# RWKV-7 layer: the next head pair's key products stand inside the triangular level loop, GpSimd splits their weights at the pair's start, ScalarE stages them level by level

## What is computed

```python
up = jnp.pad(u, ((0, 0), (1, 1), (0, 0)))
xx = 0.5 * (up[:, :-2] + up[:, 2:]) - u
xr, xw, xk, xv, xa, xg = [u + xx * mu[j] for j in range(6)]
r = heads(xr @ w_rkv[0])
k = heads(xk @ w_rkv[1])
v = heads(xv @ w_rkv[2])
...
def step(S, inp):
    r_t, w_t, k_t, v_t, a_t, b_t = inp
    sa = jnp.einsum('bhvk,bhk->bhv', S, a_t)
    S = S * w_t[:, :, None, :] + sa[..., None] * b_t[:, :, None, :] + v_t[..., None] * k_t[:, :, None, :]
    return S, jnp.einsum('bhvk,bhk->bhv', S, r_t)
```

## Time and profile before

| | us |
|---|---|
| median of three runs | 2406.75 |
| lowest and highest run | 2403.61, 2407.95 |
| the profiled execution | 2404.21 |
| its span in the trace | 2402.4 |

### The profile page before, as it was taken

One profiled execution on the slowest core, in us unless ns is written; L12 is line 12 of the kernel. 1 busy time (PEld: TensorE's weight loads), 2 busy tenths in 40 slices (PEclk: granted clock), 3 DMA queues, 4 the chain that ended last, 5 costly groups with the idle time before them and its releaser, 6 DMA issues.

```text
span 2402.4 us, 56559 instructions
## 1 busy us (share of the span) xinstructions
PE 2294.2 (95%) x24506; PEld 1851.0 (77%) x24506; DVE 1560.0 (65%) x1761; ACT 1264.5 (53%) x1400; POOL 231.8 (10%) x222
## 2 busy tenths in 40 slices
PE   8999999999999889888988889999999999999998
PEld 4677676888888466666766778888888888888886
DVE  2544776222233855555555268888888888888898
ACT  3422024222222844444444267777787778787875
POOL 2000552000000041111101130000000000000010
PEclk8999999999999989999999999999999999999999
DMA  7556225333222411111110289999999999999994
GB/s 272 193 210 245 71 88 158 88 105 87 97 97 89 144 58 59 58 58 41 54 46 20 95 321 374 365 385 361 383 361 385 360 384 358 385 363 381 360 390 174
DMA packets 228487, 511.90 MB, mean 213 GB/s; under 512 B 15271, under 2 KB 108223, under 8 KB 228031
## 3 DMA queue, kind: packets, MB, share of 16 engines
q1 hardware_dynamic: 225470, 498.61, 56.9%
q10 hardware_dynamic: 1730, 7.10, 0.8%
q0 software_dynamic: 1152, 4.19, 0.5%
HBM read 492.58 MB, written 17.30 MB: 212 GB/s over the span
## 4 chain that ended last, share of the span: by engine, by line
PE 91%; DVE 3%; issue 3%; ACT 1%; DMA 1%; POOL 0%; SPq 0%; DVEq 0%; ACTq 0%; POOLq 0%
PE bank L1673 26%; PE bank L1703 13%; PE bank L1199 3%; PE bank L1200 3%; PE bank L1201 3%; PE bank L1339 2%; PE bank L1313 2%; PE bank L1076 2%; PE bank L1105 2%; PE bank L1077 2%; PE bank L1078 2%; PE bank L1350 2%; PE bank L1217 2%; PE bank L1216 2%; PE bank L1218 2%
## 5 line engine op out<-in xcount | busy, mean ns | idle before, releaser
L3060 DVE TENSOR_TENSOR w_low<-expert_w,w_high 128x1792 fp32r<-128x1792 f32 (+2 forms) x384 | 771.9, 2024 | 120.7 <-ACT w_high L2213 118.1
L2213 ACT CAST w_high<-expert_w 128x1792 fp32r<-128x1792 f32 (+2 forms) x384 | 652.0, 1701 | 217.0 <-PE bank L1673 144.5
L1673 PE MATMUL bank<-w_high,xg_high 128*128 128x448 f32 x1024 | 294.1, 368 | 4.0 <-DVE xg_low L3050 4.0
L1673 PE MATMUL bank<-w_high,xg_low 128*128 128x448 f32 x1024 | 293.1, 367 | 0.0
L1673 PE MATMUL bank<-w_low,xg_high 128*128 128x448 f32 x1024 | 293.1, 367 | 0.0
L1673 PEld LDWEIGHTS bank<-w_high,xg_high 128*128 128x128 f32 x1024 | 191.6, 189 | 21.3 <-DVE xg_low L3050 4.1
L1673 PEld LDWEIGHTS bank<-w_high,xg_low 128*128 128x128 f32 x1024 | 192.8, 188 | 17.0
L1673 PEld LDWEIGHTS bank<-w_low,xg_high 128*128 128x128 f32 x1024 | 192.9, 188 | 15.8
L1703 PE MATMUL bank<-w_high,hid_high 128*128 128x512 f32 x448 | 175.8, 392 | 0.0
L1703 PE MATMUL bank<-w_high,hid_low 128*128 128x512 f32 x448 | 174.9, 390 | 0.0
L1703 PE MATMUL bank<-w_low,hid_high 128*128 128x512 f32 x448 | 174.7, 390 | 0.0
(11 more groups left out here) (440 smaller groups left out, 4035.1 us busy)
## 6 DMA issues: line engine op xcount, KB each, us to landing
expert_w<-in_moe_w_dram SPq DMA_DIRECT2D x128, 1792.0 KB, 9.2
expert_w<-in_moe_w_dram SPq DMA_DIRECT2D x32, 2048.0 KB, 10.4
arena<-in_mod_w_dram SPq DMA_DIRECT2D x48, 1024.0 KB, 8.2
expert_w<-in_moe_w_dram SPq DMA_DIRECT2D x32, 1536.0 KB, 9.7
arena<-in_ffn_w_dram SPq DMA_DIRECT2D x44, 512.0 KB, 5.0
slot_rows<-arena SPq DMA_DIRECT2D x25, 512.0 KB, 5.4
arena<-in_hy_w_in_dram SPq DMA_DIRECT2D x12, 1024.0 KB, 5.3
arena<-in_rw_w_rkv_dram SPq DMA_DIRECT2D x48, 256.0 KB, 2.7
```

The source lines that it names most:

```text
L1673: last = pe.matmul(bank[b0 + v][:, 0:EH], x[:, k, :], w_[:, kk, v * EH:v * EH + EH], start=(k == 0 and x is XGH and w_ is wh), stop=(k == ...
L2213: act.copy(high_piece(kind, n), piece(kind, ering[q % ERN], n // 2, n % 2))\
L3060: dve.tensor_tensor(piece(kind, low[s], n // 2, n % 2), piece(kind, ering[s], n // 2, n % 2), high_piece(kind, n).bitcast(F32), ALU.subtract)\
```

## The change

- TensorE: the 24 key products of the next pair leave their block behind the bonus sum. In each round of the level loop stand six of them (two channel tiles, three products), ahead of `level_first`. They accumulate onto bank 2. A round waits for the staged weights of its level and for the clearing of bank 2. The signal that the keys are done is given by the first transpose of `Bt` behind the loop. The waits for `score_copy_h` move from ahead of the loop into `level_first`. The first decay product moves ahead of the rates.
- VectorE: behind the first key mask it clears bank 2 with a memset of 128x512.
- ScalarE: two copies of 128x256 for each level bring the weights of two channel tiles into `stage_high` and `stage_low`. The pair for level 0 stands ahead of the score copies and waits for GpSimd's `next_digits(i)`. The others stand behind the two `first_copy` of the level before. `key_copy` moves from behind `z_copy_1` to the place behind the last `first_copy` of the loop, and reads bank 2. TensorE's `last_second` waits for it.
- GpSimd: `next_digits(i)` moves to the very start of `pair(i)`, and waits for the last state product of pair i - 1 in place of the levels of pair i.
- SP: the next pair's key weights are loaded when the keys of the pair before are done; the other weights still wait for its gate product.

The core of the diff:

```diff
-            def ahead_keys(j, tiles):
-                if tiles[0] == 0:
-                    step(pe, "ahead_pool", "next_digits", j - 1)
-                for k in tiles:
-                    mm(bank[4][:, :], keys_w_high[:, k, :], keys_high[k], start=(k == 0), stop=False)
-                    mm(bank[4][:, :], keys_w_high[:, k, :], keys_low[k], start=False, stop=False)
-                    last = mm(bank[4][:, :], keys_w_low[:, k, :], keys_high[k], start=False, stop=(k == KT - 1))
-                if tiles[-1] == KT - 1:
-                    last.then_inc(sem("ahead_products"), one("ahead_products", "keys"))
+            def ahead_keys(i, lv):
+                step(pe, "pair_vectors", "keys_cleared", i)
+                pe.wait_ge(sem("ahead_copies"), staged_keys(i + 1, lv))
+                settle(pe)
+                for n in range(2):
+                    tokens, rest = (v[n][:, bass.ds(lv * T, T)] for v in (keys_high_part, keys_low_part))
+                    for w, x in ((stage_high, tokens), (stage_high, rest), (stage_low, tokens)):
+                        mm(bank[2][:, :], w[:, n, :], x, start=False, stop=True, skip_group_check=True)
...
             def ahead_rate(j):
...
+                ahead_decay(j, 0)
                 step(pe, "pair_copies", "z_copy_1", j - 1)
...
-                for h in range(2):
-                    step(pe, "pair_copies", f"score_copy_{h}", i)
-                settle(pe)
                 with pe.Fori(0, LOOPED) as lv:
+                    if more:
+                        ahead_keys(i, lv)
                     for h in range(2):
-                        level_first(h, lv * 2 + (PER_PAIR * i + h + 1))
+                        level_first(h, lv * 2 + (PER_PAIR * i + h + 1), i)
...
+                if more:
+                    step(pe, "ahead_copies", "key_copy", i + 1)
                 for h in range(2):
                     last_second(h, i)
...
                 if more:
-                    ahead_keys(i + 1, range(KT))
                     ahead_rate(i + 1)
-                    ahead_decay(i + 1)
+                    ahead_decay(i + 1, 1)
...
+                def stage_keys(lv):
+                    act.copy(stage_high, keys_w_high[:, lv::LOOPED, :])
+                    act.copy(stage_low, keys_w_low[:, lv::LOOPED, :])\
+                        .then_inc(sem("ahead_copies"), one("ahead_copies", f"keys_staged_{lv}"))
...
+                if more:
+                    step(act, "ahead_pool", "next_digits", i)
+                    stage_keys(0)
                 for h in range(2):
                     step(act, "pair_vectors", f"joined_0_{h}", i)
...
             def pair(i, more):
+                if more:
+                    step(pool, "pair_products", "out_sum", i - 1)
+                    settle(pool)
+                    next_digits(i)
                 step(pool, "ahead_vectors", "r_1", i)
...
-                if more:
-                    pool.wait_ge(sem("level_turned"), PER_PAIR * (i + 1))
-                    next_digits(i)
...
+                    if h == 0:
+                        step(dve, "pair_vectors", "keys_masked_0", i)
+                        dve.memset(bank[2][:, :], 0.0).then_inc(sem("pair_vectors"), one("pair_vectors", "keys_cleared"))
```

64 lines of the change are left out of this document (43 added, 21 removed).

## The result

The changed kernel took 2428.86 us in the median of four runs (2425.45 to 2435.16), the kernel before 2406.84 us beside it (2403.61 to 2407.95). The ratio is 1.0102, with an interval from 1.0083 to 1.0120, so the change costs 22 us. The profiled execution of the changed kernel, 2435.16 us with a span of 2433.4 us, is the longest of its four, and its stages are read with that in mind; a second profile of the same kernel, with a span of 2421.1 us, stands beside it in the table.

What follows compares the result with a forecast made beforehand. TensorE, busy 95% of the span, was taken as the bound. Six later pairs at +0.85 us (+5.1) and the first at +11.5 gave +16.6 us: 2420.8 against 2404.21, median 2423 us, range 2412 to 2431 (8 in 10: 2409 to 2434).

Steps and rivals of the forecast that it cites:

- The first pair: Start of the first pair: TensorE waits 11.7 us for weights behind GpSimd's token subtractions; the pair in all +11.5 us.
- The removed block: From bonus product to first `wu` product: 8.15 us shrinks to 2.4 us, a gain of 5.75 us for each of seven pairs.
- A round with a group: Level loop, rounds 2 to 4: six key products with added register and wait instructions cost 1.5 us each, 4.5 us together.
- The clock: Round 2, just behind the issue gap: six products partly at 1.2 GHz, counted as 0.4 us, between -0.6 and 1.2.
- The third rival: Centring blocked in six pairs (+7 us), or two of the four groups at 1.2 GHz: 2430 to 2436 us; chance 0.10.
- The first round: Round 1 of a later pair: 1.5 us of products, 0.5 clearing wait on average, 0.5 hidden by the issue gap: +1.5 us.
- A later pair: Sum for each of six pairs after the first: -5.75 + 4.5 + 1.5 + 0.2 + 0.4 = +0.85 us.
- Nothing for centring: VectorE's centring, now overlapped by GpSimd's split, was claimed not to slow: counted as nothing.
- That the loop absorbs more: Rival: issue gap takes the whole first group and clearing wait, later rounds 0.33 us each: 2405 us; chance 0.13.
- That the first pair's wait is missing: Rival: the loop absorbs more and GpSimd reaches the split earlier, so the first pair does not wait: 2393 us; chance 0.05.
- The rival of 2427 us: Code waits not shortened at all, the loop's longer body adds nothing to hide: 0.5 us more each pair; chance 0.05.
- The gaps as waits for code: TensorE's issue gaps, 17.4 us in seven times, one in each pair's first round, look like waits for instruction fetches.

## Why the prediction was right, point by point

The direction, the range and the cause of the larger part were right. The forecast was +16.6 us, the measurement +22.0 and +22.4. The missing 5 to 6 us lie in terms that were too small, in the later rounds above all.

- **The first pair, forecast +11.5 us.** By the profile +11.5 us, from the end of the scores to the stage behind `wu` (42.9 to 54.4 us), and TensorE's new wait 11.80 us against 11.7. By the medians, 14.2 us when the old order is put back, which has a first pair 3.1 us shorter than the kernel before. The chain was right. Its emphasis on the score copies was not: the late staging freed them and won nothing, because the key group waits for the weights by itself.
- **The removed block, 5.75 us.** 8.15 to 2.67 us, 5.48 us. The remainder was taken at 2.4 us.
- **A round with a group, 1.5 us.** This is the term that was mis-sized most. Round 3 grew from 3.13 to 4.87 us, 1.74 us, and the fourth, with the 0.2 us of its head, by 1.8 us. The six products and the change over to the level's take 1.58 us; the address costs 0.15 us and the added waits about 0.1. Nothing of the 0.33 us at the head is covered: it is the loop's own.
- **The clock, 0.4 us.** The second round grew by 2.66 us. A full-clock group and its head account for 1.82, which leaves 0.84 us for the clock: 1.27 us of group at half clock (2.85 against 1.58 us), less 0.4 us that the level products behind it, now past the slow stretch for a part, win back (in the fifth pair they take 1.71 and 1.36 us in the rows, and 1.97 and 1.59 us before). The row that showed it was in the earlier trace rows, 0.65 behind the gap. I set the group behind the slow stretch for a part of the time, and it was in it, wholly or mostly, in 13 of 14 pairs. The third rival named this as two of four groups at 1.2 GHz; it was one of four. Its price was too low by its own terms: two groups at 1.5 us each, less the 0.4 us already counted, are 2.6 us a pair and 18 us in seven, 2441 us and not 2436.
- **The first round, +1.5 us.** Lead and round together +1.65 us. The parts were not right: the clearing wait is 1.05 us in a quiet pair and not 0.8. In two pairs of the six it replaces an issue gap of 2 us that the kernel before has among its scores, so the mean lead grows by 0.4 us only. The issue gaps inside the round are 2.42 and 2.34 us, not 2.76, so 0.3 to 0.4 us less where I took 0.5; that the group hid them is not shown. Without the six products the round was as long, but at a lower clock, so that run doesn't price them in this round. The round's length differs from pair to pair, from 6.1 to 9.2 us in the changed kernel.
- **`key_copy`, 0.2 us.** From the loop to the bonus product +0.46 us.
- **A later pair, forecast +0.85 us.** +2.7 and +2.1 us in two profiles, 1.4 us (0.9 to 1.9) in the medians.
- **Nothing for centring.** It keeps its 0.42 us at 1132.07, inside GpSimd's subtraction of 2.35 us from 1131.27, as the row of L2950 had suggested. The Trainium skill, "SBUF — State Buffer", section Who interferes with whom, says that a VectorE instruction with at most one input in SBUF doesn't contend with GpSimd (outside VectorE's 2-port modes), and the trace agrees.
- **The rivals.** That the loop absorbs more fell: rounds 2 to 4 grew by 2.66, 1.74 and 1.59 us, and the time by 22 us. That the first pair's wait is missing fell with the 11.80 us. That centring is blocked fell. The rival of 2427 us, in which the gaps are not shortened at all, can't be told from the forecast by the time; by the gaps the truth lies between the two, nearer to the forecast.
- **The gaps as waits for code.** That they lie 256 instructions apart speaks for it. The Trainium skill, "Runtime: NRT & Kernel Launch", section Instruction fetch mechanics, has the fetching hidden behind the running block. The traces differ here: of the first rounds of all pairs only two show no issue gap, one in the kernel with twelve products ahead of the loop (third pair) and one in that with the waits ahead of it (fourth pair).

## What to carry over

When the bound engine moves work to another place, look there for time in which it waits for another engine; a gap that it owes to its own instructions took little of the work here (0.3 to 0.9 us of 1.5 to 5.8 us put ahead of it, by the first rounds' gaps), and the fixed cost at the head of a loop took none. An experiment that leaves out dense work can also lower the clock of what stays, and then prices too little: read the granted clock beside the time. A product in a loop pays the loop's address and waits again each round, and whatever is put at the head of a loop inherits every wait of its sources: in the first pass of a pipeline ask when the slowest source, here an engine far off the bound, first delivers. And where the numbers decide what a later stage does, an experiment that changes them is read by its stages alone.

## What the hardware showed

- Six products of 128x512 in the changed kernel's loop take 1.25 to 1.27 us from the start of the first to that of the last at 2.4 GHz and 2.29 us at 1.2 GHz. In its two profiles the group of the second round, behind a gap of 1.3 to 2.9 us in the round before, ran wholly or mostly at 1.2 GHz in 13 of 14 pairs; in the 14th, behind a gap of 1.01 us, at 2.4 GHz. The gap's length alone doesn't settle it: with the staging behind the score copies three of seven ran at 2.4 GHz behind gaps of 1.6 to 2.1 us. Put half a round later, only three to five of 28 groups ran below 2.4 GHz.
- Without the 24 products the mean granted clock over the eight pairs fell to 0.91, from 0.94 and 0.95.
- TensorE's gaps put down to "issue" lie a multiple of 256 of its matmuls and weight loads apart, to within one, where no whole loop stands between them. The one in the first round was 13.9 to 19.8 us in seven to nine times between 850 and 1340 us in every version with the group ahead of the round or outside the loop (inside the round it is spread over two lines), while the instruction queue brought 107 or 108 packets of 16 KB.
- An address from a register costs TensorE's load side 147 ns for a group of six products (three instructions of 32 ns and one of 51).
- A memset of a whole bank took VectorE 485 ns, as one of that size in SBUF had the earlier trace rows, with 0.18 us of waiting for the mask that it follows.
